# The opening of a two-block transformer kernel: the first shift vector multiplied by TensorE from units that land in empty ring places, instead of accumulated by VectorE

## The reference, cut to what matters

```
mod = silu(c) @ w + b                      # c: (1, 1024), w: (1024, 3072)
shift, scale, gate = split(mod, 3)
h = rms_norm(x, g) * (1 + scale) + shift
x = x + gate * fn(h)
```

## Time and profile before

| | us |
|---|---|
| median of 3 runs | 1968.03 (1964.82 to 1968.92) |
| the profiled execution | 1972.6 |
| its span, first to last instruction | 1971.0 |
| TensorE busy | 1854.8 (94%) |
| VectorE busy | 1631.2 (83%) |
| ScalarE busy | 1150.0 (58%) |

### The profile page before, as it was taken

How to read it: one execution, slowest core, us unless ns; L and a number is a source line. 1 busy time by engine, 2 the same in 40 slices (tenths; PEclk the granted TensorE clock), 3 DMA queues, 4 the chain that set the end, 5 groups by cost and what they waited for, 6 DMA issues and landing times.

```text
span 1971.0 us, 30663 instructions
## 1 busy us (share of the span) xinstructions
PE 1854.8 (94%) x10510; PEld 1593.3 (81%) x10510; DVE 1631.2 (83%) x2124; ACT 1150.0 (58%) x1536; POOL 49.8 (3%) x56
## 2 busy tenths in 40 slices
PE   3999999988999999999999999978899999789997
PEld 2989998876788888888888888856689997679997
DVE  7999886768999898989898989888887769777554
ACT  2434444453777777777777777744554444645442
POOL 2000000000000000000000000000000000000000
PEclk8999999999999999999999999989899999899999
DMA  9978996557699999999999999958568875846762
GB/s 330 344 253 285 369 366 202 162 166 259 236 373 357 371 355 374 352 373 352 373 351 375 349 374 348 344 186 245 161 223 280 286 255 145 268 139 193 221 218 74
DMA packets 282834, 556.20 MB, mean 282 GB/s; under 512 B 30851, under 2 KB 124294, under 8 KB 282726
## 3 DMA queue, kind: packets, MB, share of 16 engines
q1 hardware_dynamic: 278352, 547.79, 80.4%
q0 software_dynamic: 2256, 5.54, 0.8%
q10 hardware_dynamic: 2118, 1.46, 0.3%
HBM read 552.58 MB, written 2.12 MB: 281 GB/s over the span
## 4 chain that ended last, share of the span: by engine, by line
PE 81%; DVE 12%; ACT 3%; issue 3%; DMA 1%; DVEq 0%; ACTq 0%; SPq 0%
PE ps L457 25%; PE ps L459 24%; PE ps L458 24%; DVE mod_acc L1792 2%; PE ps L1004 2%; ACT prob L1440 2%; DVE units_low L452 2%; PE ps L1098 1%; DVE x_tokens L1819 1%; PE ps L989 1%; DVE x_normed L1818 1%; DMA mod_in<-in_w_mod 1%; PE ps L815 1%; PE ps L977 1%; DVE act L1857 1%
## 5 line engine op out<-in xcount | busy, mean ns | idle before, releaser
L452 DVE TENSOR_TENSOR units_low<-raw_units,units_high 128x1024 fp32r<-128x1024 f32 (+1 forms) x838 | 984.6, 1217 | 132.6 <-ACT units_high L448 129.5
L448 ACT ACTIVATE units_high<-raw_units 128x1024 fp32r<-128x1024 f32 (+1 forms) x838 | 859.9, 1057 | 369.0 <-PE ps L459 333.2
L457 PE MATMUL ps<-units_high,hT_high 128*128 128x512 f32 (+1 forms) x1040 | 416.1, 400 | 3.5 <-DVE hT_low L1861 1.9
L459 PE MATMUL ps<-units_high,hT_low 128*128 128x512 f32 (+1 forms) x1040 | 408.2, 393 | 0.0
L458 PE MATMUL ps<-units_low,hT_high 128*128 128x512 f32 (+1 forms) x1040 | 406.4, 391 | 0.0
L457 PE MATMUL ps<-hT_high,units_high 128*128 128x256 f32 x1248 | 350.3, 281 | 6.4 <-DVE hT_low L1861 5.2
L459 PE MATMUL ps<-hT_high,units_low 128*128 128x256 f32 x1248 | 349.7, 280 | 0.0
L458 PE MATMUL ps<-hT_low,units_high 128*128 128x256 f32 x1248 | 349.7, 280 | 0.0
L457 PE MATMUL ps<-units_high,aT_high 128*128 128x512 f32 x632 | 251.6, 398 | 1.3 <-DVE aT_low L2046 0.7
L459 PE MATMUL ps<-units_high,aT_low 128*128 128x512 f32 x632 | 248.0, 392 | 0.0
L458 PE MATMUL ps<-units_low,aT_high 128*128 128x512 f32 x632 | 247.3, 391 | 0.0
(11 more groups left out here) (293 smaller groups left out, 1371.0 us busy)
## 6 DMA issues: line engine op xcount, KB each, us to landing
raw_units<-in_moe_w_down SPq DMA_DIRECT2D x176, 512.0 KB, 5.6
raw_units<-in_moe_w_gate SPq DMA_DIRECT2D x160, 512.0 KB, 5.4
raw_units<-in_moe_w_up SPq DMA_DIRECT2D x160, 512.0 KB, 5.5
mod_in<-in_mod_w SPq DMA_DIRECT2D x96, 512.0 KB, 6.0
mod_in<-in_w_mod SPq DMA_DIRECT2D x96, 512.0 KB, 5.5
raw_units<-in_w_gu SPq DMA_DIRECT2D x176, 256.0 KB, 3.8
raw_units<-in_w_down SPq DMA_DIRECT2D x44, 512.0 KB, 4.2
raw_units<-in_w_in SPq DMA_DIRECT2D x32, 512.0 KB, 7.9
```

The source lines that it names most:

```text
L448: eng.activation(whi[:rows, high_slot(f, n), 0:width], raw[:rows, raw_slot(f, n), 0:width], ACT.Copy).then_inc(f.hi, 1)
L452: eng.tensor_tensor(low[:rows, raw_slot(f, n), 0:width], raw[:rows, raw_slot(f, n), 0:width], whi[:rows, high_slot(f, n), 0:width].bitcast ...
L457: pe.matmul(dst, ah, bh, start=start, stop=False, **kw)
L459: return pe.matmul(dst, al, bh, start=False, stop=stop, **kw)
```

## The change: shift by TensorE, scale by VectorE

For the first block alone, the eight pieces of the shift are no longer read into `mod_in`. They are read into ring places 3 to 10 (`SHIFT0_SLOT = 3`), which are empty at the start, and TensorE multiplies them with the conditioning vector: for each of the eight units and each of its eight column blocks, the 128 x 128 block is the stationary operand and one column of `silu_c` the moving one; the sums go to eight columns of PSUM bank 2. `s_sh` counts the units that are done, and the convolution's units 3 to 10, which use the same places, wait for it on SP's queue. The bias of the shift comes in with GpSimd's small vectors (an eighth transfer) and is kept in `small`; `mod_cols` adds it. VectorE adds the eight pieces of the scale alone. SP's order is now: four pieces of the scale, four units of the shift, `x`, four units of the shift, four pieces of the scale, three units of the convolution. TensorE does four units of the shift ahead of `normed_T(0)` and four behind it. ScalarE rounds two units of the convolution ahead of `hT_high` and three among its chunks, instead of five ahead.

```diff
 V_NORM, V_C, V_CONV, V_GA, V_GF, V_GG, V_ROWS = 0, 32, 48, 72, 88, 104, 120
+V_B0 = V_ROWS
@@ mod_order
         if m == 0:
-            order += [(m, False, k, third) for third in range(2) for k in range(DC)]
+            order += [(m, False, k, 1) for k in range(DC)]
+SHIFT0_SLOT = 3
+SCALE0 = DC
@@ build
+    shift0_bias = small[:, 80:80 + DC]
+    s_sh = sem("first_shift_units_used")
@@ sync
+        def first_shift(k0, k1):
+            for k in range(k0, k1):
+                slot = SHIFT0_SLOT + k
+                sp.dma_start(raw[:, slot, :], mod_source(0)[0][k * P:(k + 1) * P, 0:D]).then_inc(fa.raw_in[slot], 16)
+
         mods(MOD_SLOTS)
+        first_shift(0, 4)
         sp.dma_start(x[:, :, :], ...).then_inc(s_x, 16)
+        first_shift(4, DC)
+        mods(SCALE0 - MOD_SLOTS)
         for k in range(CONV_UNITS_FIRST):
             issue_unit(sp, fa, N_CONV_IN, k, 0, blocks(g["conv_w_in"][0], 512)(k))
-        mods(MOD_COLS - MOD_SLOTS)
...
         for k in range(CONV_UNITS_FIRST, 32):
+            if SHIFT0_SLOT <= k < SHIFT0_SLOT + DC:
+                sp.wait_ge(s_sh, k - SHIFT0_SLOT + 1)
             issue_unit(sp, fa, N_CONV_IN, k, 0, conv_in(k) if k < 24 else conv_out(k - 24))
@@ gpsimd
+                (V_B0, DC, g["mod_b"][0, 0:1, 0:D].rearrange("a (k p) -> (a k) p", p=P))]
@@ mods_done
-        return m * (MOD_COLS + MOD_GATE) + MOD_COLS + (MOD_GATE if gate else 0)
+        return m * (MOD_COLS + MOD_GATE) + SCALE0 + (MOD_GATE if gate else 0)
@@ tensor
-        pe.wait_ge(s_vec, 16 * 7)
-        pe.transpose(ps[:, 7, 0:V_ROWS], vecs[0:V_ROWS, :], table[0:V_ROWS, C_ID:C_ID + V_ROWS]).then_inc(s_vt, 1)
+        pe.wait_ge(s_vec, 16 * 8)
+        pe.transpose(ps[:, 7, 0:P], vecs[:, :], table[:, C_ID:C_ID + P]).then_inc(s_vt, 1)
...
+        def first_shift(k0, k1):
+            for k in range(k0, k1):
+                pe.wait_ge(fa.raw_in[SHIFT0_SLOT + k], 16)
+                for c in range(DC):
+                    last = pe.matmul(ps[:, 2, c:c + 1], raw[:, SHIFT0_SLOT + k, c * P:(c + 1) * P], silu_c[:, k:k + 1],
+                                     start=k == 0 and c == 0, stop=k == DC - 1, skip_group_check=True)
+                last.then_inc(s_sh, 1)
+
+        pe.wait_ge(s_sc, 1)
+        first_shift(0, 4)
         normed_T(0)
-        pe.wait_ge(s_mused, MOD_COLS // 2)
-        sum_columns(0, 0, DC)
-        pe.wait_ge(s_mused, MOD_COLS - 2)
+        first_shift(4, DC)
+        pe.wait_ge(s_mused, SCALE0 - 2)
         for _ in range(3):
-            pe.matmul(ps[:, 2, :], ident, table[:, 0:512], start=True, stop=True)
-        pe.wait_ge(s_mused, MOD_COLS)
+            pe.matmul(ps[:, 1, :], ident, table[:, 0:512], start=True, stop=True)
+        pe.wait_ge(s_mused, SCALE0)
         sum_columns(0, DC, 2 * DC).then_inc(s_mred, 1)
@@ scalar
-        highs(fa, N_CONV_IN, 0, CONV_UNITS_FIRST)
         ac.wait_ge(s_rw, 16)
         ac.activation(rw[:, :, 0:E], rwf[:, :, :], ACT.Copy).then_inc(s_rwh, 1)
-        highs(fa, N_CONV_IN, CONV_UNITS_FIRST, AHEAD)
-        hT_high(0)
+        highs(fa, N_CONV_IN, 0, 2)
+        hT_high(0, after={c: lambda k=(c + 3) // 2: highs(fa, N_CONV_IN, k, k + 1) for c in (1, 3, 5)})
@@ vector
+        ve.tensor_copy(shift0_bias, ps[:, 7, V_B0:V_B0 + DC]).then_inc(dch, 1)
@@ mod_cols
+            if m == 0:
+                ve.wait_ge(s_sh, DC)
+                ve.tensor_tensor(mod_ab[:, 0, 1, :], ps[:, 2, 0:DC], shift0_bias, ALU.add).then_inc(s_mcol, 1)
+            else:
+                ve.tensor_copy(mod_ab[:, m % 2, 1, :], ps[:, bank, 0:DC]).then_inc(s_mcol, 1)
...
         mods(MOD_SLOTS)
         ve.wait_ge(s_x, 16)
         norm(0, 0)
-        mods(4)
+        mods(SCALE0 - MOD_SLOTS)
         lows(fa, N_CONV_IN, 0, 1)
-        mods(MOD_COLS - MOD_SLOTS - 4)
         mod_cols(0)
```

More of the change, by code:

```diff
@@ L324, in build @@
     s_vec = sem("vectors_in")
-    s_small = [sem(f"small_in{i}") for i in range(4)]
+    s_small = [sem(f"small_in{i}") for i in range(3)]
+    s_sh = sem("first_shift_units_used")
     s_vz, s_vt, s_cols, s_sc = sem("vecs_zeroed"), sem("vecsT_in_psum"), sem("cols_ready"), sem("silu_c_ready")
@@ L410, in simple, with slot_table @@
         return put
-    def slot_table(kinds, first=0):
-        seen, outv = [0] * R, []
+    def slot_table(kinds, first=0, before=(0,) * R):
+        seen, outv = list(before), []
         for n, loads in enumerate(kinds):
@@ L424, in build @@
             loads_a[N_FFN0 + k] = 2
-    in_a, seen_a = slot_table(loads_a)
+    in_a, seen_a = slot_table(loads_a, before=[16 if SHIFT0_SLOT <= i < SHIFT0_SLOT + DC else 0 for i in range(R)])
     moe_loads, moe_seen = slot_table([2 if key[0] == "gu" else 1 for key in ORDER], N_MOE)
@@ L689, in _ @@
                 (V_GF, 16, g["g_ffn_2"].rearrange("a (k p) -> (a k) p", p=P)),
-                (V_GG, 16, g["g_group_2"].rearrange("a (k p) -> (a k) p", p=P))]
+                (V_GG, 16, g["g_group_2"].rearrange("a (k p) -> (a k) p", p=P)),
+                (V_B0, DC, g["mod_b"][0, 0:1, 0:D].rearrange("a (k p) -> (a k) p", p=P))]
         for at, n, src in rows:
@@ L1369, in mod_gate, with hT_high @@
                 .then_inc(s_mga, 1)
-        def hT_high(s):
+        def hT_high(s, after=None):
             ac.wait_ge(s_mcol, s + 1)
@@ L1384, in hT_high @@
                     .then_inc(s_hth, 1)
+                if after is not None and c in after:
+                    after[c]()
         def squares(before):
@@ L1771, in _ @@
         ve.wait_ge(s_vt, 1)
+        ve.tensor_copy(shift0_bias, ps[:, 7, V_B0:V_B0 + DC]).then_inc(dch, 1)
+        chain[0] += 1
         ve.tensor_copy(cols[:, :], ps[:, 7, 0:V_ROWS]).then_inc(s_cols, 1)
@@ L1782, in mods @@
                 m, gate, k, third = MOD_ORDER[q]
-                if not gate and (k, third) == (0, 0):
+                if not gate and (k, third) == (0, 1 if m == 0 else 0):
                     ve.wait_ge(*((s_bias3, 16) if m == 3 else (s_bias, 16 * (MAIN_COLS.index(m) + 1))))
@@ L1801, in mod_cols @@
                                     in1=norm_gain(m), op0=ALU.add, op1=ALU.mult)
-            ve.tensor_copy(mod_ab[:, m % 2, 1, :], ps[:, bank, 0:DC]).then_inc(s_mcol, 1)
+            if m == 0:
[3 more added lines that the diff above has]
+                ve.tensor_copy(mod_ab[:, m % 2, 1, :], ps[:, bank, 0:DC]).then_inc(s_mcol, 1)
         def residual(s, f=None, end=None):
```

## The result

| | before | changed |
|---|---|---|
| median (22 runs each, taken side by side) | 1966.05 us | 1970.97 us |
| the profiled execution | 1972.6 | 1967.98 |
| its span | 1971.0 | 1966.3 |
| first product of `conv_in` | 46.97 | 55.42 |

The ratio of the times is 1.0031, with a 95% interval of 1.002 to 1.0042: the change costs 6.1 us (3.9 to 8.3; the ratio of the two medians alone, 1.0025, lies inside). The two spans say the opposite, and the last part of the explanation shows why a single execution can't decide here. What is sharp in one trace is the start of `conv_in`, and that is 8.45 us later.

The account below looks back on a forecast made before the run. TensorE was taken to bound the kernel, its largest hole being the opening. `conv_in` starting at 42.7 against 46.97 (4.3 us) plus 0.2 for the clock gave -4.5 us: median 1968.0 to 1963.5, range 1960 to 1977.5.

Parts of the forecast that it names:

- First four units, 64 instructions. If the clock rises after some 5 us of this stream: TensorE's first shift half: 24 instructions in the low clock (5.0 us), 40 in the high one (4.6), done at 24.3.
- leave TensorE no idle time: Argument against the clock staying low in the shift's stream: its weight loads keep TensorE busy; no size given.
- Rival 1: Shift's stream on TensorE stays in the low clock, 0.21 us each; `conv_in` at 54.7, 7.7 us late, 1975.7; chance 0.40.
- the low stretch of the earlier trace: TensorE's low clock from 48.3 to 51.7, behind a pause; 0.2 us gain counted for the chance it isn't repeated.
- Rival 2: Clock rises only with the transposes, or load rate doesn't follow it; `conv_in` at 46.3, 0.7 early, 1967.3; chance 0.15.
- Transfers, VectorE, ScalarE: Opening queues besides TensorE: `x` squared from about 20.7, last scale addition ending at 32.7, unit 0's rest taken by 35.1.
- without TensorE's part `conv_in` could start at about 38: Opening: with transfers, VectorE and ScalarE alone, `conv_in` starts at about 38, 9 us early.
- One for one: Behind the opening: a microsecond won or lost before `conv_in`'s first product at 46.97 is one at the end.

Follow-up runs that it names:

- experiment 1: Changed kernel with seven identity products put into TensorE's waits ahead of the shift's stream; ratio to the kernel before 1.0027, `conv_in` start 50.20.
- experiment 6: Changed kernel with the shift products' operands exchanged (`silu_c` column stationary, unit moving, 32 instructions for 128); ratio to the kernel before 0.9992, start 46.24.
- experiment 3: Changed kernel with only the first of eight column blocks multiplied in each of the last four shift units; 1956.82 us, ratio to the kernel before 0.9965.
- experiment 8: experiment 5 with four units each, TensorE's in the form of experiment 6, ScalarE's row copy behind the norm, three identity products; 1958.43 us, ratio 0.9953.
- experiment 4: Changed kernel with the shift's units landing in the ring in the same order, but VectorE adding them; ratio to the kernel before 0.9991, start 42.90.
- experiment 5: Changed kernel with `x` behind the first four scale pieces, TensorE multiplying three shift units, VectorE adding five, two identity products; 1959.16 us, ratio 0.9974.
- experiment 9: The changed kernel run and profiled once more, unedited; 1973.35 us, ratio to the kernel before 1.0035, start 55.72.
- experiment 7: experiment 4 with `x` loaded ahead of the shift's units, VectorE adding all sixteen pieces; ratio to the kernel before 0.9987, start 45.12.
- experiment 2: Changed kernel without the three identity products (six instructions) behind the shift's stream; one run, 1974.66 us, start 52.10.

## Why the prediction was wrong

**The step that failed** is "First four units, 64 instructions. If the clock rises after some 5 us of this stream": it did not rise, in this half or the other. The forecast took 0.115 us for most of the 128 instructions; that price is right, but only at 2.4 GHz (0.107 in experiment 1), and this stream neither reaches that level (changed kernel, twice) nor keeps it when given (experiment 1). The argument for it, that the loads "leave TensorE no idle time", doesn't decide: in experiment 6 TensorE is no busier (without a gap in both) and its clock rises. That it would rise was taken over from transposes, a stream of another form. And the earlier trace rows, from which the price came, show four one-column products amid dense ones; such a row gives the price at the clock that its neighbours brought about, and tells nothing about what a long stream of the kind does to the clock.

**Rival 1 came true step by step.** Its ends of stages were 28.1, 31.5, 44.9 and 49.9; measured 28.31, 31.75, 45.27 and 50.51, then 4.9 to `conv_in` where 4.8 was taken. Its price of 0.21 was 0.213; the identity products took 5.24 instead of 5.0; its start of 54.7 was 55.42. It is also right on the time within the interval: 7.7 late was forecast, 6.1 (3.9 to 8.3) measured. Of the lag of 8.45 us, 1.1 is gone by 60 us: the low stretch of the earlier trace rows is in the profile of before and not in the one after. The prediction had counted 0.2 for it. What else comes back can't be read from these two profiles (last part). The error was the choice between the two, 0.45 and 0.40; this rival's sum holds.

**Rival 2 falls** in both its forms. The clock did not rise with the transposes in the changed kernel, and where it rose behind them ahead of a full second half, at 31.00 in experiment 1, it fell again at 34.41. And the price follows the clock: 0.107 and 0.21 us from start to start in the two stretches of experiment 1, where the loads' records last 192 and 333 ns, as in the earlier trace rows. The Trainium skill, "TensorE: Matmul & The Clock Gate", "LDWEIGHTS (loading the stationary operand)", gives 107 ns for 128 columns: that is the spacing in the high clock, and half of the spacing in the low one.

**Transfers, VectorE, ScalarE** were right within 0.9 us, and hidden. `x` was first squared at 21.30 (forecast 20.7), the scale's last addition ended at 33.56 (32.7), unit 0's rest at 35.80 (35.1). No unit was late for TensorE in `conv_in`. The sentence that without TensorE's part `conv_in` could start at about 38 is borne out as far as the runs go: 40.01 with part of the stream gone (experiment 3), 40.95 with all of the work done (experiment 8), both still with TensorE last.

**"One for one"** holds within what the runs can tell. Start and time against before: experiment 3, -7.0 and -6.9; experiment 4, -4.1 and -1.8 (-5.9 to +2.6); experiment 5, -3.7 and -5.1 (-8.8 to -1.4); experiment 1, +3.2 and +5.3 (2.2 to 8.6); the change, +8.45 and +6.1 (3.9 to 8.3), and again (experiment 9) +8.75 and +6.9 (2.6 to 11.2); experiment 8, -6.0 and -9.2 (-12.4 to -6.1). Experiments 6 and 7, -0.7 and -1.9, are too small to tell. The change and experiment 8 lie 0.1 to 0.2 outside their intervals, and the start of the kernel before is known from one execution.

**Why the profile after is the shorter one.** Span less the start of `conv_in` is 1924.0 in the profile of before, 1910.9 in that of after, 1917.5 in experiment 9, and between 1911.0 and 1920.9 in the eight others, though the instructions behind that point are alike. The profiled executions of before and after stand at the two ends of a scatter of 13 us. Most of it is found by following the same instruction, counted from the first product of `conv_in`, through two traces. The changed kernel's lag falls from 7.3 to 2.7 us while the kernel before goes from 152 to 328 us, from 2.7 to -0.6 around 488 (the low stretch of the earlier trace rows, which the profile after doesn't have, lies there), and from -0.9 to -4.6 behind 1800. In the first and the last of these stretches TensorE's granted clock is 1.00 in both traces and it has next to no gap, and still the products of 256 columns follow one another every 0.118 us in one execution and every 0.113 in the other. So 50 us hold 359 products of the kernel before and 369 of the changed one (columns as in the earlier trace rows):

```profile
200.00:250.00 50.00, 50.00 (x359) 46.98 (x358) 44.80 (x42) 22.11 (x24) 0.00 (x0) 1.00 1.02 369
207.30:257.30 50.00, 50.00 (x369) 47.05 (x368) 46.53 (x43) 22.85 (x25) 0.00 (x0) 1.00 1.05 385
```

The spacing holds for a whole stage, and it isn't the kernel's: in the stage from 1425 to 1625 us it is 0.113 in the first profile of the changed kernel and 0.118 in experiment 9, and this makes 4.6 of the 6.6 us by which the second falls behind after the start of `conv_in`. What sets it isn't settled; these stages are far from anything changed.

## What to carry to other kernels

A matrix-vector product on TensorE with the matrix as the stationary operand is a stream of weight loads: price it at the low clock, and expect what follows it to start low too. Make the matrix the moving operand (experiment 6), and give TensorE only as much as ends before the other inputs arrive (experiment 8). When a change has two halves, here earlier landing and another engine, cost and run them apart: one was worth 4.1 us of start (2.5 by VectorE, the rest by TensorE's clock), the other cost 12.5. And don't judge a change of some us in 1970 by two single traces: here their spans had the wrong sign.

## What was not expected of the hardware

- TensorE's clock fell twice within a stream of one-column products with no idle time (17.34 and 34.41 in experiment 1).
- The same instructions up to 31.6 us gave a rise of the clock behind the transposes in experiment 3 (identity products 2.82) and none in the changed kernel (5.40, and 5.47 in experiment 9). Of the ten profiles in which these sixteen transposes begin in the low clock, six show a rise at their end or within 0.6 us behind it (the kernel before, experiments 1, 3, 4, 6 and 7), four don't (the changed kernel, experiments 2, 5 and 9). The Trainium skill, "TensorE: Matmul & The Clock Gate", "PE-mode transpose", says that transposes don't bring the high clock; experiment 4, where TensorE did nothing else from 13.97 until `sum_columns` ran in 2.05 us, speaks against it, those without a rise don't. What decides is open.
- At a granted clock of 1.00 and without a gap, products of 256 columns follow one another every 0.113 or every 0.118 us, for a whole stage, and which of the two differs between executions of one kernel.
